# The low parts of 22 weight units move from VectorE to GpSimd, and the final norm's chunks are put between them

## The chip, the cores and the metric

One core of one Trainium2 chip runs the whole program. The metric is the device time in microseconds (us). The engines are named as in the profile: PE is TensorE (PEld its weight loads), DVE VectorE, ACT ScalarE, POOL GpSimd, SP SyncE.

## The reference

Two blocks of two layers each, float32, model width 1024, 256 tokens. The first block has feed-forward layers and two mixers, and ends with a final norm. The second puts 16 meta tokens ahead (272 rows) and runs `hybrid_layer` twice; the change lies here:

```python
def hybrid_layer(x, ...):
    h = rms_norm_2(x, norm_g)
    z = h @ w_in
    aq, ak, av, ag, mq, mk, mv, mi, mf, mo, mgate = jnp.split(z, split_points(), axis=-1)
    ...
    ya = sliding_window_sink_attention(q, k, v, sink) * jax.nn.silu(ag)
    ...
    hm = mlstm_chunkwise(mq, mk, mv, log_i, log_f)
    ym = rms_norm_2(hm, out_norm_g) * jax.nn.sigmoid(mo) * jax.nn.silu(mgate)
    y = jnp.concatenate([ya, ym], axis=-1) @ w_out
    return x + y
```

The attention has 16 heads of 64, the mLSTM 4 heads (q and k of 128, v of 256).

## The kernel before

Every weight matrix is cut into units of 512 rows by 256 columns (128 partitions x 4 x 256 in SBUF); there are 456. A unit U passes through four engines: SP loads it into `raw[U % 4]`; ACT copies it, rounded, into the high part `w_hi` (L1124, semaphore `hi_made`); DVE subtracts the two and leaves the low part `w_lo` (L1862, `split_w`, semaphore `lo_made`); PE multiplies hi by the activations' high and low parts and lo by the high part (L690). In the second block the high and low parts have five slots, of which one lies in `y_both`, so that a group named `y_both<-raw` is the same work as `w_lo<-raw`. The slot of `raw` is loaded again once the low part is made.

Units 320 to 371 and 388 to 439 are the streams of the two hybrid layers: 52 units each, numbered u = 0 to 51 below, in the order kv, mif, aq, mqk, mv, mo, ag, mg. Behind each come 16 units of the projection (u = 52 and on). All engines walk through the same list; in step u, ACT and DVE make the parts of unit u + 4 (`split_ahead`, `units_ahead`). A table `VISITS` says which pieces of attention and mLSTM each step does beside its unit: attention in u = 18 to 34 (`att`), the four mLSTM heads in u = 34 to 51 (`ml`, stages 0 to 3 of head k in steps 34, 36, 37, 39 plus 4k).

One mLSTM head is a loop over the engines. Its lines, as the prediction names them: ACT takes squares of PE's sums (L1558, L1560), PE sums those (L1056), DVE adds (L2446), ACT takes a root (L1578, with a table load at L1156 before it), DVE inverts (L2458) and scales (L2469), DVE makes the next head's matrix (L2420, L2432, L2434) for PE (L1047). The gates of mo, ag and mg run in between on the same engines: DVE scales a tile from PSUM (L1899), multiplies (L2451, L2481, then L2489 or L2494), ACT rounds the result into `y_both` (L1594), DVE makes its low part (L2504). DVE and ACT run everything in the written order.

GpSimd in these steps scales attention rows (L1808, L1810) and, behind all visits of layer 0, multiplies the eight chunks of `h` for the final norm (L1838, L1839, chained by `link`); DVE waits for them (`h_final`) only in the projection.

Of the kernel before, what the change touches and what calls it, by code (L numbers as in the profile page):

```python
# [192 lines left out]
    return U - RING - 1  # L193


def units_ahead(U):

    u = U - FIRST_STREAM
    if u < CATCH_UP:
        return (U + LEAD,)  # L200
    return (U + LEAD, U + LEAD + 1) if u == CATCH_UP else (U + LEAD + 1,)
# [51 lines left out]
def build_stack(nc: bass.Bass, consts, x, ffn1_norm, ffn1_w_in, ffn1_w_out, mix_norm, ffn2_norm, ffn2_w_in, ffn2_w_out,  # L253
# [12 lines left out]
    with ExitStack() as ctx:  # L266
# [3 lines left out]
        def sem(name):  # L270
            return ctx.enter_context(nc.semaphore(name))
# [37 lines left out]

        ident, tri = cst("ident"), cst("tri")  # L310

        def hi_part(U):
            s = parts_slot(U)
            return parts_5[0] if s == RING else w_hi[:, s]

        def lo_part(U):
            s = parts_slot(U)
            return parts_5[1] if s == RING else w_lo[:, s]
# [82 lines left out]
        w_loaded = [sem(f"w_loaded{i}") for i in range(RING)]  # L401
        hi_made = sem("hi_made")
        lo_made = sem("lo_made")
        unit_done = sem("unit_done")
        first_done = sem("first_done")
        tile_read = sem("tile_read")
# [104 lines left out]
        def _(sp):  # L511
# [23 lines left out]
            def load(U, src, wait):  # L535

                n = UNITS[U][3]
                if wait is not None:
                    sp.wait_ge(lo_made, wait)
                sp.dma_start(raw[:, U % RING, 0:n, :], src).then_inc(w_loaded[U % RING], 16)  # L540

# [17 lines left out]
            def straight(name, first=0):  # L559
                ub, pb, npairs = PHASES[name]  # L560
                for p in range(first, npairs):
                    for U in units_before(name, p):
                        src, l, k0, n, c0 = UNITS[U]
                        a = dram[src][l]
                        if name == "out01":

                            for dst, s_ in small[2 * (U - ub):2 * (U - ub) + 2]:
                                sp.dma_start(dst, s_).then_inc(sg_loaded, 16)
                        if name.startswith("mif"):

                            sp.wait_ge(lo_made, U - RING + 1)
                            for g in range(2):
                                sp.dma_start(raw[:, U % RING, 0:n, 32 * g:32 * g + 4],
                                             a[k0 * P:(k0 + n) * P, c0 + 4 * g:c0 + 4 * g + 4].rearrange(
                                                 "(k p) n -> p k n", p=P)).then_inc(w_loaded[U % RING], 16)
                            continue
                        load(U, a[k0 * P:(k0 + n) * P, c0:c0 + CU].rearrange("(k p) n -> p k n", p=P),
                             U - RING + 1 if U >= RING else None)
# [56 lines left out]
        def _(pe):  # L635
# [12 lines left out]
            def unit(U, k0, n, pair, npair_off, xs, N, first, last, ready, off, tiles=2, wide_x=False,  # L648
                     mid=None, both=False):


                pe.wait_ge(lo_made, U + 1 + off)
                hi_w, lo_w = hi_part(U), lo_part(U)
                accs = [bank[tile_bank(2 * pair + m, off)] for m in range(tiles)]

                def bank_free(m):

                    T = 2 * pair + m
                    if T in BANK_OF:
                        pe.wait_ge(gates_sig, 2 * NC8)  # L660
                        if T >= 2 * PHASES["sg_out"][1]:
                            pe.wait_ge(sg_read, NC8)
                        if BANK_OF[T] < 4:
                            pe.wait_ge(tile_read, T - 7)
                    elif T in FIRST_BANK and isinstance(off, int) and off == 0:
                        pe.wait_ge(tile_read, T - 7)
                    elif not isinstance(off, int):
                        pe.wait_ge(halves_added, TURNED[T] - 3 + tile_off(off))
                    elif not (T - 3 + off // 2 <= 0):
                        pe.wait_ge(tile_read, T - 3 + tile_off(off))  # L670

                for j in range(n):
                    k = k0 + j
                    if ready is not None:
                        pe.wait_ge(act_ready, ready + k + 1)
                    a, b = (k * L + META, (k + 1) * L) if N == SEQ and wide_x else (k * N, (k + 1) * N)
                    begin, end = first and j == 0, last and j == n - 1
                    residual = 2 * pair in T_OUT
                    if both:
                        kinds = ((hi_w, xs[:, :, a:b], slice(0, 2 * N)), (lo_w, xs[:, 0, a:b], slice(N, 2 * N)))  # L680
                    else:
                        kinds = tuple((w, xs[:, i, a:b], slice(0, N)) for w, i in ((hi_w, 0), (hi_w, 1), (lo_w, 0)))
                    for g, (w, moving, cols) in enumerate(kinds):
                        final = end and g == len(kinds) - 1
                        for m in range(tiles):
                            if begin and g == 0:
                                bank_free(m)
                                if residual and BANK_OF[2 * pair + m] < 4:
                                    add_residual(2 * pair + m)
                            i_ = mm(accs[m][:, cols], w[:, j, m * P:(m + 1) * P], moving,  # L690
                                    start=begin and g == 0 and not residual, stop=final)
                            if final and m == 0 and tiles == 2:
                                i_.then_inc(first_done, 1)
                    if j == n // 2 - 1 and mid is not None:
                        mid()
                i_.then_inc(unit_done, 1)
# [984 lines left out]
        def _(pool):  # L1681
# [113 lines left out]
            for l in range(DEPTH):  # L1795
# [16 lines left out]
                def turn(c):  # L1812
# [13 lines left out]
                    if c == NC8:  # L1826
                        pool.wait_ge(qc_new, n + 1)
                        pool.wait_ge(rs_new, l + 1)
                        nc.gpsimd.memset(k_up[:, :, :], 0.0).then_inc(padded, 1)

                for u in range(STREAM_UNITS):
                    for kind, n in VISITS[u]:
                        if kind in ("att", "turn"):
                            dict(att=att, turn=turn)[kind](n)
                if l == 0:
                    pool.wait_ge(final_r, 1)
                    for c in range(NC8):
                        link(nc.gpsimd.tensor_scalar(h[:, c, META:L], h[:, c, META:L], pcol("final_norm", c), None, MUL))  # L1838
                        TT(h[:, c, META:L], h[:, c, META:L], sq[:, META:L], MUL).then_inc(h_final, 1)  # L1839
                    pool.wait_ge(h_final, NC8)  # L1840
                    h_squares(7, "proj0", 0)

# [2 lines left out]
        def _(dve):  # L1845
# [10 lines left out]
            def split_w(U, off=0):  # L1856

                if U >= NU:
                    return
                n, s = UNITS[U][3], U % RING  # L1860
                dve.wait_ge(hi_made, U + 1 + off)
# [795 lines left out]
```

## Time and profile before

| | |
|---|---|
| median of 3 runs | 1449.24 us (1448.88 to 1450.42) |
| the profiled execution's own time | 1448.88 us |
| its span in the profile | 1447.1 us |
| PE busy | 1432.7 us, 99% of the span |
| DVE busy | 1092.7 us, 76% |
| ACT busy | 853.7 us, 59% |
| POOL busy | 273.1 us, 19% |

The span is 1.8 us shorter than the execution's own time. A busy share is an average over stages. In the timeline an instruction that waits for access to its operands is still shown as running, so its duration against that of its like tells of such a wait.

### The profile page before, as it was taken

What the parts mean: (1) busy time and instruction counts of PE and PEld (TensorE: products, weight loads), DVE (VectorE), ACT (ScalarE), POOL (GpSimd) and SP (SyncE); (2) the same over time, 40 slices, a digit from 0 to 9 for tenths busy, and PEclk for the clock granted to TensorE, in tenths of its full rate; (3) what the DMA queues carried; (4) which work ended last, traced back from release to release, by engine and by line L of the source; (5) the groups of instructions that cost most, each with busy time, mean ns of one, the idle gap of its engine ahead of it and who ended that gap; (6) DMA issues with size and microseconds to landing.
All of it is one profiled execution on the core that took longest, in us unless ns stands there. A gap on an engine that the chain in (4) does not pass through costs nothing.

```text
span 1447.1 us, 27343 instructions
## 1 busy us (share of the span) xinstructions
PE 1432.7 (99%) x9657; PEld 1321.4 (91%) x9657; DVE 1092.7 (76%) x2021; ACT 853.7 (59%) x1559; POOL 273.1 (19%) x329
## 2 busy tenths in 40 slices
PE   8999999999999999999999999999999999999998
PEld 7888899988888888889988888999999999999998
DVE  6777679877756777667787766898778779976883
ACT  6665458766544666446566554656757555576762
POOL 1111113121102111014031113332250035121000
PEclk9999999999999999999999999999999999999999
DMA  6667754556565656565456565554345555434533
GB/s 211 196 196 211 233 180 131 186 179 202 183 188 182 191 187 198 186 195 164 159 171 201 181 188 175 164 145 124 88 127 142 164 153 155 134 94 124 147 118 117
DMA packets 247875, 241.25 MB, mean 167 GB/s; under 512 B 15456, under 2 KB 246736, under 8 KB 247784
## 3 DMA queue, kind: packets, MB, share of 16 engines
q1 hardware_dynamic: 244888, 236.73, 53.8%
q10 hardware_dynamic: 2896, 3.30, 0.8%
q8 instruction: 58, 0.95, 0.3%
q14 instruction: 33, 0.27, 0.1%
HBM read 238.92 MB, written 1.07 MB: 166 GB/s over the span
## 4 chain that ended last, share of the span: by engine, by line
PE 87%; DVE 7%; ACT 3%; issue 2%; DMA 1%; ACTq 0%; SPq 0%; DVEq 0%
PE bank L690 78%; DVE w_lo L1862 2%; DVE work L2458 1%; PE bank L989 1%; ACT w_hi L1124 1%; PE bank L1007 1%; PE bank L972 1%; PE bank L918 1%; DMA raw<-in_w_out_dram 1%; PE bank L928 1%; DVE work L1899 1%; DVE work L2481 1%; DMA raw<-in_ffn_w_in_dram 1%; PE bank L988 1%; ACT L1156 0%
## 5 line engine op out<-in xcount | busy, mean ns | idle before, releaser
L690 PE MATMUL bank<-x_both,w_hi 128*128 128x512 f32 (+2 forms) x3216 | 748.1, 336 | 0.6 <-DVE h L1962 0.5
L1862 DVE TENSOR_TENSOR w_lo<-raw,w_hi 128x1024 fp32r<-128x1024 f32 (+1 forms) x429 | 519.4, 1234 | 203.3 <-ACT w_hi L1124 202.2
L1124 ACT CAST w_hi<-raw 128x1024 fp32r<-128x1024 f32 (+1 forms) x429 | 429.3, 1028 | 125.4 <-PE bank L690 108.3
L690 PEld LDWEIGHTS bank<-x_both,w_hi 128*128 128x128 f32 x3216 | 468.0, 189 | 3.5 <-DVE w_lo L1862 1.1
L690 PEld LDWEIGHTS bank<-x_both,w_lo 128*128 128x128 f32 x2312 | 406.1, 189 | 62.7
L690 PE MATMUL bank<-x_both,w_lo 128*128 128x256 f32 (+1 forms) x2312 | 462.4, 281 | 0.0
L690 PE MATMUL bank<-y_both,w_hi 128*128 128x512 f32 (+2 forms) x1376 | 331.5, 342 | 1.8 <-DVE w_lo L1862 1.1
L690 PEld LDWEIGHTS bank<-y_both,w_lo 128*128 128x128 f32 x1040 | 184.3, 188 | 31.3
L690 PE MATMUL bank<-y_both,w_lo 128*128 128x256 f32 (+1 forms) x1040 | 206.1, 280 | 0.0
L690 PEld LDWEIGHTS bank<-y_both,w_hi 128*128 128x128 f32 x1376 | 200.3, 189 | 2.8 <-DVE w_lo L1862 1.8
L1749 POOL TENSOR_TENSOR work<-work,rstd 128x256 f32<-128x256 f32 x88 | 67.0, 783 | 412.7 <-ACT work L1193 412.7
L1175 ACT COPY pre<-bank 128x256 f32<-128x256 f32 x176 | 56.7, 374 | 67.1 <-PE bank L690 66.8
L1205 ACT CAST y_both<-work 128x256 f32 (+1 forms) x88 | 32.7, 406 | 59.7 <-DVE work L1930 59.5
L690 PE MATMUL bank<-x_both,y_both 128*128 128x272 f32 (+1 forms) x504 | 67.6, 290 | 0.0
L1193 ACT ACTIVATE work<-work 128x256 f32<-128x256 f32 x88 | 33.2, 418 | 53.4 <-DVE work L1919 53.4
L1135 ACT ACTIVATE x_both<-h,par 128x256 fp32r<-128x256 f32 (+1 forms) x56 | 28.2, 513 | 61.2 <-DVE h L1975 52.9
L690 PEld LDWEIGHTS bank<-x_both,y_both 128*128 128x128 f32 x504 | 63.6, 188 | 0.6
L1810 POOL TENSOR_SCALAR work<-work 128x256 f32<-128x256 f32 x32 | 36.4, 1137 | 99.2 <-DVE work L2381 99.2
L1714 POOL TENSOR_TENSOR sq<-h 128x256 f32<-128x256 f32 (+1 forms) x34 | 21.4, 631 | 163.2 <-DVE h L1975 162.9
L1879 DVE SCALAR_TENSOR_TENSOR x_both<-h,par,x_both 128x256 fp32r<-128x256 f32 (+1 forms) x56 | 29.1, 528 | 24.8 <-ACT x_both L1135 24.6
L1937 DVE TENSOR_TENSOR y_both<-work,y_both 128x256 f32 (+1 forms) x88 | 33.6, 423 | 15.3 <-ACT y_both L1205 14.7
L1899 DVE TENSOR_TENSOR work<-bank,rstd 128x256 f32<-128x256 f32 (+1 forms) x98 | 37.5, 422 | 6.8 <-PE bank L690 6.5
(312 smaller groups left out, 1397.9 us busy)
## 6 DMA issues: line engine op xcount, KB each, us to landing
raw<-in_ffn_w_in_dram SPq DMA_DIRECT2D x176, 512.0 KB, 3.8
raw<-in_w_in_dram SPq DMA_DIRECT2D x100, 512.0 KB, 3.7
raw<-in_ffn_w_out_dram SPq DMA_DIRECT2D x64, 512.0 KB, 4.6
raw<-in_w_out_dram SPq DMA_DIRECT2D x32, 512.0 KB, 4.0
raw<-in_ffn_w_out_dram SPq DMA_DIRECT2D x32, 384.0 KB, 3.4
raw<-in_rec_w_in_dram SPq DMA_DIRECT2D x16, 512.0 KB, 4.4
raw<-in_sg_w_in_dram SPq DMA_DIRECT2D x16, 512.0 KB, 4.1
raw<-in_rec_w_out_dram SPq DMA_DIRECT2D x8, 512.0 KB, 3.5
```

The costliest lines, as they stand in the source:

```text
L690: i_ = mm(accs[m][:, cols], w[:, j, m * P:(m + 1) * P], moving, start=begin and g == 0 and not residual, stop=final)
L1124: nc.scalar.copy(hi_part(U)[:, 0:n, :], raw[:, s, 0:n, :]).then_inc(hi_made, 1)
L1135: i_ = activation(xview(dst, k, N), src, ACT.Copy, scale=scale)
L1175: nc.scalar.copy(ffn_b[:, m, :], bank[b][:, SEQ:2 * SEQ]).then_inc(low_copied, 1)
L1193: activation(ffn_s[:, m, :], ffn_t[:, m, :], ACT.Silu).then_inc(silu_done, 1)
L1205: nc.scalar.copy(dst, ffn_h[:, m, :]).then_inc(act_hi, 1)
L1749: TT(ffn_r[:, m, :], ffn_s[:, m, :], rstd[:, META:L], MUL).then_inc(gate_scaled, 1)
L1810: TS(pr[:, P:AW], pr[:, P:AW], rec[:, 1:2], None, MUL).then_inc(s_prob, 1)
L1862: TT(lo_part(U)[:, 0:n, :], raw[:, s, 0:n, :], hi_part(U)[:, 0:n, :].bitcast(fp32), SUB).then_inc(lo_made, 1)
L1879: i_ = STT(out=xview(dst_lo, k, N), in0=src, scalar=scale, in1=hi, op0=MUL, op1=SUB)
L1899: TT(dst, tile(pr, m, N), rstd[:, T0:L], MUL).then_inc(tile_read, 1)
L1937: TT(lo, ffn_h[:, m, :], hi.bitcast(fp32), SUB).then_inc(act_ready, 1)
```

## The change

Eleven units of each stream (u = 23, 26, 29, ... 53, the last of them in the projection) get their low part from GpSimd. DVE skips them. GpSimd makes each in the step four before (19, 22, ... 49), after that step's attention work, and counts them on a semaphore of its own, `lo_by_pool`; PE and SP wait on that one for these units and on `lo_made` for the rest. The eight chunks of the final norm, which stood behind the last visit of layer 0, now stand one in each of the steps 36 to 43, behind the step's low part.

```diff
+POOL_UNITS = [FIRST_STREAM + l * (STREAM_UNITS + 16) + u for l in range(DEPTH) for u in range(23, 54, 3)]
+
+def parts_made(U):
+
+    made = sum(V < U for V in POOL_UNITS)
+    return (1, made + 1) if U in POOL_UNITS else (0, U + 1 - made)
...
+        def wait_parts(engine, U):
+            by_pool, count = parts_made(U)
+            engine.wait_ge(lo_by_pool if by_pool else lo_made, count)
...
@@ block.sync, load @@
-                if wait is not None:
+                if wait is not None and isinstance(wait, int):
+                    wait_parts(sp, wait - 1)
+                elif wait is not None:
                     sp.wait_ge(lo_made, wait)
...
@@ block.tensor, unit @@
-                pe.wait_ge(lo_made, U + 1 + off)
+                if isinstance(off, int):
+                    wait_parts(pe, U + off)
+                else:
+                    pe.wait_ge(lo_made, U + 1 + off)
...
@@ block.gpsimd @@
+                def low_part(U):
+
+                    if U in POOL_UNITS:
+                        pool.wait_ge(hi_made, U + 1)
+                        TT(lo_part(U), raw[:, U % RING], hi_part(U).bitcast(fp32), SUB).then_inc(lo_by_pool, 1)
+
                 for u in range(STREAM_UNITS):
                     for kind, n in VISITS[u]:
                         if kind in ("att", "turn"):
                             dict(att=att, turn=turn)[kind](n)
-                if l == 0:
-                    pool.wait_ge(final_r, 1)
-                    for c in range(NC8):
+                    low_part(FIRST_STREAM + l * (STREAM_UNITS + 16) + u + LEAD + 1)
+                    if l == 0 and 36 <= u < 36 + NC8:
+                        c = u - 36
+                        if c == 0:
+                            pool.wait_ge(final_r, 1)
                         link(nc.gpsimd.tensor_scalar(h[:, c, META:L], h[:, c, META:L], pcol("final_norm", c), None, MUL))
                         TT(h[:, c, META:L], h[:, c, META:L], sq[:, META:L], MUL).then_inc(h_final, 1)
+                if l == 0:
                     pool.wait_ge(h_final, NC8)
                     h_squares(7, "proj0", 0)
...
@@ block.vector, split_w @@
                 if U >= NU:
                     return
+                if U in POOL_UNITS:
+                    return
```

In the changed file the lines stand further down: GpSimd's L1838 and L1839 are L1865 and L1866 there, the new low part is L1854, DVE's L1862 is L1892 and its lines behind that are 30 higher.

GpSimd's queue in layer 0, from the end of its attention work into the mLSTM steps, before:

```order
L1810 TENSOR_SCALAR work<-work 128x256 [waits s_rec] x8
L1838 TENSOR_SCALAR h<-h,par 128x256 [waits final_r]
L1839 TENSOR_TENSOR h<-h,sq 128x256 [waits pool_ch]
L1838 TENSOR_SCALAR h<-h,par 128x256
L1839 TENSOR_TENSOR h<-h,sq 128x256 [waits pool_ch]
```

and of the change, from the low part of u = 38 on:

```order
L1854 TENSOR_TENSOR w_lo<-raw,w_hi 128x1024 [waits hi_made]
L1865 TENSOR_SCALAR h<-h,par 128x256 [waits final_r]
L1866 TENSOR_TENSOR h<-h,sq 128x256 [waits pool_ch]
L1854 TENSOR_TENSOR w_lo<-raw,w_hi 128x1024 [waits hi_made]
L1865 TENSOR_SCALAR h<-h,par 128x256
L1866 TENSOR_TENSOR h<-h,sq 128x256 [waits pool_ch]
L1865 TENSOR_SCALAR h<-h,par 128x256
L1866 TENSOR_TENSOR h<-h,sq 128x256 [waits pool_ch]
L1865 TENSOR_SCALAR h<-h,par 128x256
L1866 TENSOR_TENSOR h<-h,sq 128x256 [waits pool_ch]
L1854 TENSOR_TENSOR y_both<-raw,y_both 128x1024 [waits hi_made]
L1865 TENSOR_SCALAR h<-h,par 128x256
```

Chunk 0 now stands behind the low part of u = 38, chunks 1 to 3 behind that of u = 41, chunks 4 to 6 behind that of u = 44 and chunk 7 behind that of u = 47.

DVE's queue in layer 1 around step 40, before, from the tiles of step 39 to the low part of u = 45:

```order
L1899 TENSOR_TENSOR work<-bank,rstd 128x256 [waits unit_done]
L2451 SCALAR_TENSOR_TENSOR work<-work 128x256 [waits gate_act] x2
L2481 SCALAR_TENSOR_TENSOR work<-work 128x256 [waits gate_act] x2
L2489 SCALAR_TENSOR_TENSOR work<-work 128x256 [waits s_out,dch]
L2489 SCALAR_TENSOR_TENSOR work<-work 128x256
L1862 TENSOR_TENSOR w_lo<-raw,w_hi 128x1024 [waits hi_made]
L2504 TENSOR_TENSOR y_both<-work,y_both 128x256 [waits act_hi] x2
L2441 TENSOR_TENSOR work<-work 128x272 [waits floor_loaded,m_dsq,m_num]
L1862 TENSOR_TENSOR w_lo<-raw,w_hi 128x1024 [waits hi_made]
```

and of the change:

```order
L1929 TENSOR_TENSOR work<-bank,rstd 128x256 [waits unit_done]
L2481 SCALAR_TENSOR_TENSOR work<-work 128x256 [waits gate_act] x2
L2511 SCALAR_TENSOR_TENSOR work<-work 128x256 [waits gate_act] x2
L2519 SCALAR_TENSOR_TENSOR work<-work 128x256 [waits s_out,dch]
L2519 SCALAR_TENSOR_TENSOR work<-work 128x256
L2534 TENSOR_TENSOR y_both<-work,y_both 128x256 [waits act_hi] x2
L2471 TENSOR_TENSOR work<-work 128x272 [waits floor_loaded,m_dsq,m_num]
L1892 TENSOR_TENSOR w_lo<-raw,w_hi 128x1024 [waits hi_made]
```

The low part of u = 44 is gone from behind the gate's products; that of u = 45 stays.

## Rows read from the trace of the kernel before

**Rows 1.** The page: busy time of each engine, and the chain by engine

```profile
PE 1432.7 (99%) x9657; PEld 1321.4 (91%) x9657; DVE 1092.7 (76%) x2021; ACT 853.7 (59%) x1559; POOL 273.1 (19%) x329
...
PE 87%; DVE 7%; ACT 3%; issue 2%; DMA 1%; ACTq 0%; SPq 0%; DVEq 0%
```

**Rows 2.** Windows of 10 us: PE, PEld, DVE, ACT, POOL busy, granted clock, DMA

```profile
1360.00:1370.00 10.00, 9.28 (x70) 8.68 (x69) 9.84 (x22) 6.70 (x15) 0.00 (x0) 1.00 0.43 119
1380.00:1390.00 10.00, 9.09 (x70) 8.57 (x69) 9.84 (x22) 5.43 (x13) 0.00 (x0) 1.00 0.53 162
1400.00:1410.00 10.00, 8.94 (x76) 8.73 (x75) 7.88 (x14) 6.23 (x9) 0.00 (x0) 1.00 0.29 80
...
1120.00:1130.00 10.00, 9.61 (x74) 9.24 (x73) 7.39 (x16) 7.78 (x15) 0.00 (x0) 1.00 0.50 157
1150.00:1160.00 10.00, 9.50 (x76) 9.29 (x75) 6.40 (x11) 4.39 (x7) 4.16 (x6) 1.00 0.75 248
```

**Rows 3.** The chain that ended last, layer 0 and layer 1: start, us, what

```profile
1093.00 1.86 DVE work L2458
...
1357.05 1.86 DVE work L2458
...
1366.99 0.44 DVE work L2489
1367.45 0.67 ACT y_both L1594 x2
...
1374.32 1.86 DVE work L2458
```

**Rows 4.** Timeline of POOL: start, us, engine, line, operation

```profile
1057.48 0.92 POOL L1838 TENSOR_SCALAR h<-h,par 128x256 f32<-128x256 f32 x1
1058.49 0.73 POOL L1839 TENSOR_TENSOR h<-h,sq 128x256 f32<-128x256 f32 x1
...
1191.44 0.78 POOL L1825 TENSOR_TENSOR work<-work 128x272 f32<-128x272 f32 x1
```

**Rows 5.** Timeline of DVE and of POOL, layer 1, query turns beside low parts

```profile
1201.23 1.22 DVE L1862 TENSOR_TENSOR w_lo<-raw,w_hi 128x1024 fp32r<-128x1024 f32 x1
1202.37 1.69 DVE L1862 TENSOR_TENSOR y_both<-raw,y_both 128x1024 fp32r<-128x1024 f32 x1
...
1201.46 1.51 POOL L1824 TENSOR_TENSOR work<-work,con 128x272 f32<-128x272 f32 x1 [3.11 <-DVE work L2312]
1202.93 1.76 POOL L1825 TENSOR_TENSOR work<-work 128x272 f32<-128x272 f32 x1
```

**Rows 6.** Timeline of ACT and of DVE, layer 1, step 40

```profile
1348.71 1.03 ACT L1124 CAST w_hi<-raw 128x1024 fp32r<-128x1024 f32 x1
...
1349.73 0.76 DVE L2489 SCALAR_TENSOR_TENSOR work<-work 128x256 f32<-128x256 f32 x2
1350.40 1.22 DVE L1862 TENSOR_TENSOR w_lo<-raw,w_hi 128x1024 fp32r<-128x1024 f32 x1
```

**Rows 7.** Timeline of ACT and of DVE, layer 1, step 43

```profile
1361.79 1.04 ACT L1124 CAST w_hi<-raw 128x1024 fp32r<-128x1024 f32 x1
...
1363.08 0.74 DVE L2504 TENSOR_TENSOR y_both<-work,y_both 128x256 fp32r<-128x256 f32 x2
```

**Rows 8.** Timeline of ACT and of DVE, layer 1, step 46

```profile
1375.71 1.04 ACT L1124 CAST w_hi<-raw 128x1024 fp32r<-128x1024 f32 x1
...
1377.15 0.76 DVE L2481 SCALAR_TENSOR_TENSOR work<-work 128x256 f32<-128x256 f32 x2
```

**Rows 9.** Timeline of DVE, layer 1, step 49

```profile
1387.30 1.23 DVE L1862 TENSOR_TENSOR w_lo<-raw,w_hi 128x1024 fp32r<-128x1024 f32 x1
1388.44 0.75 DVE L1899 TENSOR_TENSOR work<-bank,rstd 128x256 f32<-128x256 f32 x2
```

**Rows 10.** Timeline of POOL and of DVE, attention of layer 0

```profile
1004.78 1.02 POOL L1810 TENSOR_SCALAR work<-work 128x256 f32<-128x256 f32 x1 [2.83 <-DVE work L2381]
...
1009.18 0.16 DVE L2380 TENSOR_TENSOR work<-work 128x2 f32<-128x2 f32 x1
```

More of the change, by code:

```diff
@@ L403, in build_stack @@
         lo_made = sem("lo_made")
+        lo_by_pool = sem("lo_by_pool")
         unit_done = sem("unit_done")
@@ L569, in straight @@
                         if name.startswith("mif"):
-                            sp.wait_ge(lo_made, U - RING + 1)
+                            wait_parts(sp, U - RING)
                             for g in range(2):
```

## The prediction

> **What bounds the kernel now.** I read the page first: PE is busy 99% of the span, and 87% of the chain that ended last is PE [rows 1]. So the most that any change off PE can give is what PE waits. The windows say where that is: five stretches of 10 us, all at the end of a stream, in which PE is busy 9.28, 9.09, 8.94, 9.61 and 9.50 of 10 [rows 2]; the missing parts sum to 0.72 + 0.91 + 1.06 + 0.39 + 0.50 = 3.6 us. In two of them DVE is busy 9.84 of 10. Then the chain: in both layers it leaves PE in the mLSTM steps and goes round DVE and ACT, once per head. DVE inverts at 1357.05 and again at 1374.32, a loop of 17.27 us, and within it goes straight from DVE's gate product (L2489) to ACT's rounding (L1594) [rows 3]. ACT takes its squares behind that, and PE's L1056 waits for them. So there are two regimes. In attention and in the projections' bulk PE is the bound and DVE has room. In steps 38 to 52 of each stream the bound is the DVE and ACT loop: a microsecond more or less on DVE between two inversions is a microsecond of the end, once PE's small cover is used up, and at both layers' ends it is, since PE waits there.
>
> **What the change removes.** 22 low parts leave DVE. The next instruction starts 1.14 us behind such a one [rows 5], so DVE sheds 25 us of work. Which of them are on the loop decides. Six of eleven per layer (u = 23 to 38) are made in steps 19 to 34, attention. There DVE waits for ACT's exponentials anyway: worth nothing. The other five are made in steps 37, 40, 43, 46 and 49, in the loop.
>
> **What it adds.** First the operation's own time. GpSimd takes 0.73 us for a product of 256 columns and 0.78 for 272 [rows 4]; it never did 1024 columns or this rounded output. If 0.16 us of it is fixed, as DVE shows for two columns [rows 10], the rest grows fourfold: 0.16 + 4 x 0.57 = 2.4 us. Bounds: nothing fixed, 4 x 0.73 = 2.9; half fixed, 0.37 + 4 x 0.37 = 1.8. I take 2.4. GpSimd has room: its work share is 19% [rows 1], and PE needs each part four steps later, over 10 us.
>
> The Trainium skill (GPSIMD Engine Reference, section 3.1) gives 4497 ns for a float32 tensor_tensor of 2048 columns; half of it, an estimate from that page, is 2.25 us. By it the sum below would be 0.9 us lower.
>
> Second, the lock. GpSimd's L1824 starts at 1201.46 while DVE's low part runs, and takes 1.51 us, where its like take under 0.8; it ends at 1202.97. DVE's next low part starts at 1202.37 and takes 1.69 instead of 1.22: the other's rest was 0.60, it lost 0.47, so a blocked instruction loses the rest less 0.13. GpSimd's next one (1202.93) again takes 1.76 [rows 5]. So they exclude each other for whole instructions, and take turns: GpSimd, waiting first, went ahead of the DVE instruction queued behind. DVE instructions with one operand in PSUM do not seem to take part. The price is then not the 1.1 us that DVE sheds but what stands behind the 2.4 us that GpSimd holds.
>
> The Trainium skill (SBUF — State Buffer, section SBUF: two separate sides) says that a DVE instruction with two SBUF inputs and a GpSimd instruction that reads SBUF share an exclusive lock, and that the later one fully blocks. By that rule the sum is the one below; without a lock it would be the first rival. The trace agrees with its 1.69 us for 1.22.
>
> **Where each low part lands**, from layer 1 (layer 0 has the same order):
> - Attention: GpSimd is free at 1005.80 and would run to 1008.2; DVE's next instruction with two SBUF operands is at 1009.18 [rows 10]. Cost 0. After the double step 22 it falls on later ones, but with PE's slack of some microseconds there.
> - Step 37: DVE's tile scaling (PSUM, not blocked) may start earlier, but PE's tile is only just done: -0.3, bounds 0 and -1.1.
> - Step 40: ACT ends the high part of u = 44 at 1349.74. DVE starts the first of two gate products at 1349.73 and the second right behind [rows 6]. GpSimd waits for the first, then goes ahead of the second: +2.25 (2.4 less 0.13). The low part shed here (1350.40) stood behind L1594's release and off the loop: nothing comes back. L1594, the squares, the next high part and PE's L1056 are late by all of it.
> - Step 43: the high part is ready at 1362.83, while DVE makes the low part of u = 46. GpSimd goes next and holds up L2504, due at 1363.08 [rows 7]: +2.25, less the 1.13 of the low part shed before the tiles: +1.1.
> - Step 46: ready at 1376.75, GpSimd runs to 1379.25. L2481 was due at 1377.15 [rows 8]: +1.95. Less 1.13 is +0.8; ACT's next high part is late by the full 1.95 and then sets DVE's low part of u = 51: +1.0.
> - Step 49: DVE's low part (1387.30) stood between the loop and the tiles at 1388.44 [rows 9]; the tiles read PSUM: -1.15.
>
> Sum per layer -0.3 + 2.25 + 1.1 + 1.0 - 1.15 = +2.9; both layers +5.8.
>
> **The final norm's chunks** (layer 0 alone) ran in steps 36 to 39, beside DVE work that PE covered. Each is 0.92 + 0.73 us of GpSimd [rows 4]. Chunks 1 to 3 now run behind the low part of u = 41, beside L2420 and L2481: +0.3. Chunks 4 to 6 follow that of u = 44, where DVE has L2504 twice and L2441: turns of 0.92, 0.73 and 0.92 less 0.13 each are 2.2, the fourth turn ahead of the low part of u = 45 adds 0.6, and 1.3 is idle time in which DVE waited for that unit's high part: +1.5. Chunk 7 takes one turn: +0.8. Together +2.6, bounds 0 and 4.0. The final norm itself is due only in the projection, and is early enough.
>
> SP's loads wait for parts that are ready up to 3 us later, with more than 5 us to spare before ACT needs them: 0. PE and SP get no more instructions.
>
> Total +8.4. Against the profiled execution's own 1448.88 (span 1447.1) that is 1457.3; the median stood 0.36 above it, and I forecast 1457.4.
>
> **Bounds.** The operation's time enters six blocks (steps 40, 43, 46 twice): 6 x -0.6 = -3.6 and 6 x +0.5 = +3.0. Chunks: -2.6 to +1.4. Low end 1457.3 - 6.2 = 1451.1, high end 1461.7.
>
> **Rivals.**
> - No lock between these two forms, or so short that it doesn't matter (for it: most of the low parts beside GpSimd's work show small differences; against: [rows 5]). Then steps 37, 43, 46 and 49 shed 3.7 us per layer from the loop, and PE stops waiting: at most the 3.6 us of [rows 2], 1445.3. It decides if a low part on DVE beside GpSimd's stays at 1.22. Chance 0.10.
> - The lock is real but the blocks miss the loop. The point is step 40: if GpSimd starts 0.75 us later than I think, both gate products have passed, and 2.25 per layer go away: +3.9 in all; if the chunks find DVE waiting too, +1.3, which is 1450.2. Against it: [rows 6], start and end within 0.01 us, and either order ends at the same time. Chance 0.14.
> - The main case, DVE blocked on its loop: 0.76, of which some 0.04 lies above the range through effects in attention (a GpSimd row scaling late by a low part, and PE's transposes with it).
>
> This kernel's runs tell a change from none at about 0.2%, 2.9 us. The main case is slower, the second rival within, the first faster. The range must leave out the first rival and a little at the top: 1450.5 to 1462.5.
>
> **What would show it.** In the profile after: GpSimd's low parts at 2.4 us when alone. DVE's busy time down by less than 25 us, since blocked instructions count as running. The second L2519 of step 40 (L2489 before) at about 2.7 us instead of 0.43, L2534 in step 43 and L2511 in step 46 likewise. PE's waits before its squares' sum (L1056 before) up from under 1 us to 1 to 4 us in the last three heads of both layers, the loop of 17.27 us at 19 or more for heads 1 to 2 and 18.4 for the next, and the attention steps unchanged. I am wrong if these blocks are short, if DVE goes ahead of a waiting GpSimd, or if GpSimd's operation takes much less or more than 1.8 to 2.9 us.

## The result, and the profile after

The changed kernel takes 1455.13 us (median of 6 runs, 1453.82 to 1455.98), the kernel before 1449.21 us in the same series (6 runs, 1448.56 to 1450.42). The ratio is 1.004, with a 95% interval of 1.003 to 1.005: slower by 5.9 us. The profiled execution took 1454.83 us, its span is 1453.0 us. Forecast were 1457.4 us and "slower"; the time lies in the range.

The page of the changed kernel first, its line of busy times and the group of GpSimd's low parts:

```profile
PE 1432.9 (99%) x9657; PEld 1321.0 (91%) x9657; DVE 1084.8 (75%) x1999; ACT 853.8 (59%) x1559; POOL 326.0 (22%) x351
...
L1854 POOL TENSOR_TENSOR w_lo<-raw,w_hi 128x1024 fp32r<-128x1024 f32 x18 | 44.8, 2487 | 88.1 <-ACT w_hi L1143 88.1
```

DVE lost 22 instructions that take 1.14 us each from start to start, 25 us, but its busy time fell by only 7.9 us against [rows 1]: the rest is DVE standing in front of a lock, which counts as running. Then the waits of PE (line, for whom, us in total, times, longest), after:

```profile
PE bank L1075 <- ACT work L1577: 5.5, 4, 1.7
PE bank L1066 <- DVE work L2464: 3.3, 2, 1.9
```

In the kernel before, the first of these was

```profile
PE bank L1056 <- ACT work L1558: 2.0, 3, 0.9
```

and the second was not there. Both lie in the mLSTM steps at the ends of the two streams.

The loop of the heads shows where. DVE's inversion (L2458 before, L2488 after) stands once in each head. The timeline of DVE, the kernel before, layer 0 and layer 1 (the inversions of [rows 3] not repeated), and one row of attention in layer 1 for the offset:

```profile
1075.46 1.85 DVE L2458 RECIPROCAL work<-work 128x272 f32<-128x272 f32 x1 [1.26 <-ACT work L1578]
1110.54 1.85 DVE L2458 RECIPROCAL work<-work 128x272 f32<-128x272 f32 x1 [1.51 <-ACT work L1578]
1133.46 1.84 DVE L2458 RECIPROCAL work<-work 128x272 f32<-128x272 f32 x1
...
1248.13 0.17 DVE L2381 RECIPROCAL work<-work 128x2 f32<-128x2 f32 x1
1339.79 1.85 DVE L2458 RECIPROCAL work<-work 128x272 f32<-128x272 f32 x1 [1.42 <-ACT work L1578]
...
1396.91 1.84 DVE L2458 RECIPROCAL work<-work 128x272 f32<-128x272 f32 x1
```

and the same of the changed kernel:

```profile
1075.18 1.85 DVE L2488 RECIPROCAL work<-work 128x272 f32<-128x272 f32 x1 [0.96 <-ACT work L1597]
1095.49 1.85 DVE L2488 RECIPROCAL work<-work 128x272 f32<-128x272 f32 x1 [1.50 <-ACT work L1597]
1114.04 1.85 DVE L2488 RECIPROCAL work<-work 128x272 f32<-128x272 f32 x1 [1.51 <-ACT work L1597]
1136.67 1.84 DVE L2488 RECIPROCAL work<-work 128x272 f32<-128x272 f32 x1
...
1251.68 0.17 DVE L2411 RECIPROCAL work<-work 128x2 f32<-128x2 f32 x1
...
1343.06 1.85 DVE L2488 RECIPROCAL work<-work 128x272 f32<-128x272 f32 x1 [1.06 <-ACT work L1597]
1362.52 1.85 DVE L2488 RECIPROCAL work<-work 128x272 f32<-128x272 f32 x1 [1.04 <-ACT work L1597]
1380.19 1.85 DVE L2488 RECIPROCAL work<-work 128x272 f32<-128x272 f32 x1 [1.50 <-ACT work L1597]
...
1402.51 1.84 DVE L2488 RECIPROCAL work<-work 128x272 f32<-128x272 f32 x1
```

The reader takes the distance between two inversions in each list and subtracts. Through attention the two executions keep one distance: the changed one is 0.17 us early in layer 0 and 3.55 late in layer 1 (1251.68 less 1248.13), so its layer 0 had cost 3.7 by then. The one exception seen is two rows of layer 0 (L2411 at 1001.03 and 1004.88), 0.36 us late behind a low part of GpSimd; at the next row, 1009.22, the distance is back. From there:

| | predicted | layer 0 | layer 1 |
|---|---|---|---|
| up to the first inversion (step 37) | -0.3 | -0.11 | -0.28 |
| first to second (step 40) | +2.25 | +2.77 | +2.20 |
| second to third (step 43) | +1.1 | +1.01 | +0.40 |
| third to fourth (steps 46, 49) | +1.0 - 1.15 | -0.29 | -0.27 |
| behind the fourth, to the end | 0 | +0.34 | +0.30 |
| sum | +2.9, and +2.6 for chunks in layer 0 | +3.7 | +2.35 |

Layer 0 has the chunks in it. Now the blocks, as the text calls the time that an instruction stands in front of the lock. The timelines of POOL and of DVE in step 40 of layer 1, changed kernel:

```profile
1353.08 2.60 POOL L1854 TENSOR_TENSOR w_lo<-raw,w_hi 128x1024 fp32r<-128x1024 f32 x1 [11.52 <-ACT w_hi L1143]
...
1352.99 2.97 DVE L2519 SCALAR_TENSOR_TENSOR work<-work 128x256 f32<-128x256 f32 x2
...
1357.44 0.44 DVE L2471 TENSOR_TENSOR work<-work 128x272 f32<-128x272 f32 x1 [0.58 <-ACT work L1579]
1358.31 1.22 DVE L1892 TENSOR_TENSOR w_lo<-raw,w_hi 128x1024 fp32r<-128x1024 f32 x1 [0.43 <-ACT w_hi L1143]
```

Beside [rows 6]: the pair L2519 took 0.76 us and now takes 2.97. The second of the pair began 0.34 in, so it took 2.63 where it takes 0.42. Step 43 of layer 1 went otherwise:

```profile
1368.38 3.17 POOL L1854 TENSOR_TENSOR w_lo<-raw,w_hi 128x1024 fp32r<-128x1024 f32 x1 [12.70 <-ACT w_hi L1143]
...
1367.41 1.20 DVE L1892 TENSOR_TENSOR y_both<-raw,y_both 128x1024 fp32r<-128x1024 f32 x1
1368.54 0.74 DVE L2534 TENSOR_TENSOR y_both<-work,y_both 128x256 fp32r<-128x256 f32 x2
1369.21 0.74 DVE L1929 TENSOR_TENSOR work<-bank,rstd 128x256 f32<-128x256 f32 x2
1369.88 2.28 DVE L2481 SCALAR_TENSOR_TENSOR work<-work 128x256 f32<-128x256 f32 x2
```

GpSimd was shown as running from 1368.38, but both L2534 (0.74 us, as always) passed it. Its 3.17 us are 0.8 of waiting and 2.4 of work, and of this only what outlasted the tiles from PSUM fell on DVE: L2481 (L2451 before) took 2.28 instead of 0.74, 1.54 us. Less the 1.14 of the low part shed that is +0.40. In layer 0 the same block is followed by chunk 7:

```profile
1102.98 2.27 DVE L2481 SCALAR_TENSOR_TENSOR work<-work 128x272 f32<-128x272 f32 x2
1105.17 0.98 DVE L2511 SCALAR_TENSOR_TENSOR work<-work 128x272 f32<-128x272 f32 x2
1106.18 1.24 DVE L2519 SCALAR_TENSOR_TENSOR work<-work 128x272 f32<-128x272 f32 x2
...
1078.01 1.36 DVE L2511 SCALAR_TENSOR_TENSOR work<-work 128x272 f32<-128x272 f32 x2
...
1077.98 0.74 POOL L1866 TENSOR_TENSOR h<-h,sq 128x256 f32<-128x256 f32 x1
1088.54 1.39 POOL L1865 TENSOR_SCALAR h<-h,par 128x256 f32<-128x256 f32 x1
...
1091.92 1.14 POOL L1866 TENSOR_TENSOR h<-h,sq 128x256 f32<-128x256 f32 x1
```

L2511 and L2519 lost 0.2 and 0.45 us there, 0.65 for chunk 7. The L2511 of 1.36 us is that of step 38, beside the second half of chunk 3: it takes 0.79 alone, so chunk 3 cost 0.57, which is all by which layer 0's +2.77 exceeds layer 1's +2.20. The last two POOL rows are of chunks 4 and 5: with these it was mostly GpSimd that waited (0.92 and 0.73 us alone).

### The profile page after: what moved, and what is told of

The parts are those of the page before. It is cut to its first block, busy times and chain, and to the rows that moved or that the text cites. A ratio compares the mean times of both kernels' runs of the same rounds, so it can differ in the third digit from the quotient of the medians.

```text
span 1453.0 us, 27343 instructions
## 1 busy us (share of the span) xinstructions
PE 1432.9 (99%) x9657; PEld 1321.0 (91%) x9657; DVE 1084.8 (75%) x1999; ACT 853.8 (59%) x1559; POOL 326.0 (22%) x351
## 4 chain that ended last, share of the span: by engine, by line
PE 90%; DVE 5%; ACT 2%; issue 2%; DMA 1%; ACTq 0%; SPq 0%; DVEq 0%
PE bank L709 81%; DVE w_lo L1892 1%; PE bank L1008 1%; PE bank L1026 1%; DVE work L2488 1%; PE bank L991 1%; PE bank L937 1%; PE bank L947 1%; DVE work L2519 1%; DMA raw<-in_ffn_w_in_dram 1%; ACT w_hi L1143 1%; PE bank L1007 1%; PE bank L1066 1%; DVE work L1929 0%; PE bank L1027 0%
## 5 line engine op out<-in xcount | busy, mean ns | idle before, releaser
L1892 DVE TENSOR_TENSOR w_lo<-raw,w_hi 128x1024 fp32r<-128x1024 f32 (+1 forms) x411 | 497.5, 1235 | 202.4 <-ACT w_hi L1143 201.7
L1854 POOL TENSOR_TENSOR w_lo<-raw,w_hi 128x1024 fp32r<-128x1024 f32 x18 | 44.8, 2487 | 88.1 <-ACT w_hi L1143 88.1
```

Source lines behind the costliest of these rows:

```text
L1854: TT(lo_part(U), raw[:, U % RING], hi_part(U).bitcast(fp32), SUB).then_inc(lo_by_pool, 1)
L1892: TT(lo_part(U)[:, 0:n, :], raw[:, s, 0:n, :], hi_part(U)[:, 0:n, :].bitcast(fp32), SUB).then_inc(lo_made, 1)
```

## The experiments

All twelve are built on the changed kernel and timed against the kernel before on the same chip; "against before" is the difference to its median in that series (1448.6 to 1450.0 us). The changed kernel's own is +5.9. Between two series the differences to before are compared, not the bare medians. Where a run's file has one to three lines more, its line numbers are that much higher (L2521 in experiment 6 is L2519).

**1. Only attention's low parts** (the list `range(23, 54, 3)` of units cut):

```diff
-POOL_UNITS = [... for u in range(23, 54, 3)]
+POOL_UNITS = [... for u in range(23, 39, 3)]
```

> The changed kernel with only the six low parts per layer that are made in attention (u = 23 to 38, steps 19 to 34) on GpSimd; the five in the mLSTM steps go back to DVE. My theory: attention costs nothing, so the time is that of the kernel before, 1449.2 us, within 1. In the changed kernel the high parts stood 0.17 us early all through layer 0's attention and a constant 3.55 late all through layer 1's, which is what the theory rests on. Rival: part of the 5.9 us is made in attention, by GpSimd scaling rows later: 1451 to 1453.

Measured: 1448.66 us, ratio 0.9999 (0.9990 to 1.0008). Attention costs nothing and gives nothing, though DVE sheds 12 low parts there. The chunks keep their new places in this run, and with no low part ahead of them they cost nothing either.

**2. The same places, one input.** The low parts of these 22 units are left out (they are zero).

```diff
-TT(lo_part(U), raw[:, U % RING], hi_part(U).bitcast(fp32), SUB).then_inc(lo_by_pool, 1)
+nc.gpsimd.tensor_scalar(lo_part(U), raw[:, U % RING], 0.0, None, MUL).then_inc(lo_by_pool, 1)
```

> The changed kernel with the same 22 instructions on GpSimd at the same places and waits, but each reads one tensor (a TENSOR_SCALAR of raw times 0) instead of two: the low parts of these units are left out of the products (they are zero). Theory of the lock between instructions with two operands in SBUF: in the changed kernel L1865, a TENSOR_SCALAR, ran beside DVE's low part (1091.22, 1.24 us) and beside L2450 without holding either up, so here the blocks of L2519, L2511 and L2481 go away, at whatever length the GpSimd instruction has, and DVE is rid of 22 low parts: 1445.3 to 1447 us. Rival: any long GpSimd instruction on SBUF keeps DVE out, or the loss comes from the order of waits and not from a lock: 1454 or more.

Measured: 1446.54 us, ratio 0.9984 (0.9975 to 0.9993). Queue, waits and places are those of the changed kernel, and GpSimd's instruction is even longer (2.77 us alone), yet the loss is gone and turns into a gain of 2.4 us. So the loss hangs on what GpSimd's instruction is, not on the waits or the order. The run changes its operation together with the number of its inputs; which of the two decides is not separated here. Step 40 of layer 1, DVE and POOL:

```profile
1349.14 1.60 DVE L2519 SCALAR_TENSOR_TENSOR work<-work 128x256 f32<-128x256 f32 x2
...
1349.24 2.96 POOL L1854 TENSOR_SCALAR w_lo<-raw 128x1024 fp32r<-128x1024 f32 x1 [11.12 <-ACT w_hi L1143]
```

L2519 loses 0.84 us, not 2.2: this instruction keeps DVE out for a part of its time only, and its last 1.5 us run beside DVE's next ones. It is not free, though: L2511 in step 46 took 1.32 us for 0.75, and L2481 in step 43 0.92 for 0.74. That the blocks would go away at any length, as I expected, did not hold.

**3. Step 40 alone undone**, and **4. the same with the chunks back in step 36.**

```diff
-... for u in range(23, 54, 3)]
+... for u in range(23, 54, 3) if u != 44]
```

> The changed kernel with one unit per layer (u = 44, made in step 40) back on DVE, so 20 low parts on GpSimd instead of 22. My theory: the block of the second L2519 (2.63 us instead of 0.42) is the whole price of step 40, 2.2 us per layer, and the later steps stay as they are: 1455.1 - 4.4 = 1450.7 us, within 1. Rival: the loop is bound elsewhere too (ACT's table loads, PE's sums), so that a block taken away shows only in part, or the next block grows by as much: 1453 to 1455.

Measured: 1452.23 us, ratio 1.0023 (1.0014 to 1.0033), 3.3 against before. That is 2.6 less than the changed kernel (2.9 by the bare medians), not 4.4. In the trace layer 1 gave 1.9 back and layer 0 only 1.15; from first to second inversion it was the full 2.2 in layer 1. The timelines of layer 0 there show the chunks, which used to run in the shadow of the low part's block, now taking turns with DVE on the loop:

```profile
1081.90 2.17 POOL L1865 TENSOR_SCALAR h<-h,par 128x256 f32<-128x256 f32 x1
...
1082.94 0.98 DVE L2534 TENSOR_TENSOR y_both<-work,y_both 128x272 fp32r<-128x272 f32 x2
...
1086.58 1.35 DVE L2511 SCALAR_TENSOR_TENSOR work<-work 128x272 f32<-128x272 f32 x2
```

> The changed kernel with u = 44 back on DVE and, as well, the chunks all in step 36. Taking away u = 44 alone gave 2.9 us where 4.4 were expected: in layer 1 1.9 of the 2.2, in layer 0 only 1.15. In that run's trace GpSimd's chunks, which had run while the low part's block kept DVE waiting, now took turns with DVE's own instructions from step 38 on (L2534 0.63 for 0.43, L2511 1.00 for 0.43). Theory: without them layer 0 gains what layer 1 does: 1454.2 (chunks alone back) less 2 x 1.9 = 1450.4, 1449.6 to 1451.2. Rival: in layer 0 the block of step 40 was partly covered by PE's slack whatever the chunks do: 1451.5 to 1452.5.

Measured: 1449.46 us, ratio 1.0001 (0.9993 to 1.0010). That is just below my range of 1449.6 to 1451.2. Against the run that has only the chunks back (experiment 5) it is 5.3 less (4.7 by the bare medians). From first to second inversion the step itself gives 2.2 us in either layer when the chunks are out of the way. With step 40 and the chunks' spread undone, nothing of the slowdown is left that can be measured.

**5. The chunks alone back in step 36.**

```diff
-if l == 0 and 36 <= u < 36 + NC8:
-    c = u - 36
-    if c == 0:
-        pool.wait_ge(final_r, 1)
-    link(...); TT(...)
+if l == 0 and u == 36:
+    pool.wait_ge(final_r, 1)
+    for c in range(NC8):
+        link(...); TT(...)
```

> The changed kernel with the eight chunks of the final norm all in step 36, ahead of the low part of u = 41, where they ran in the kernel before. By the recorded prediction their spreading costs 2.6 us: 1452.5. By the trace of the changed kernel layer 0 cost 3.7 and layer 1, which has no chunks, 2.4: 1.3 at most for the chunks, of it 0.65 at chunk 7 (L2511 0.63 for 0.43 and L2519 0.89 for 0.43 us); chunks 4 to 6 ran while GpSimd, not DVE, waited. So 1453.9, 1453.3 to 1454.6. In the trace the shift against the kernel before should grow equally in both layers.

Measured: 1454.18 us, ratio 1.0036 (1.0022 to 1.0050). That is 5.6 against before, 0.3 under the changed kernel's, with intervals that overlap, so the times alone show no gain; the trace is finer: layer 0 cost 2.5 us in place of 3.7. So by the traces the spread costs 1.2 us, not 2.6. Layer 1 ended 0.7 later than in the changed kernel, all of it behind its last head, which I can't explain.

**6. GpSimd waits for both products in step 40.**

```diff
 pool.wait_ge(hi_made, U + 1)
+if (U - FIRST_STREAM) % (STREAM_UNITS + 16) == 44:
+    pool.wait_ge(act_new, 16 + 16 * l + 4)
```

> The changed kernel, in which GpSimd's low part of u = 44 (step 40) waits until DVE has made the gate's second product, so that this product is never held up. The prediction's second rival took it that 2.25 us per layer would then go away: 1455.1 - 4.4 = 1450.7. My theory now is that DVE runs in order and every one of its instructions with two SBUF operands ahead of the tiles is on the loop: L2534 is held up in place of L2519, and only the idle time behind it is saved (0.58 us ahead of L2471 and 0.43 ahead of the next low part, since ACT's rounding comes earlier), about 1.0 per layer: 1453.1, from 1452.3 to 1454.

Measured: 1453.15 us, ratio 1.0029 (1.0019 to 1.0040), 4.6 against before. The timeline of DVE, step 40 of layer 1:

```profile
1352.14 0.76 DVE L2521 SCALAR_TENSOR_TENSOR work<-work 128x256 f32<-128x256 f32 x2
1353.04 2.95 DVE L2536 TENSOR_TENSOR y_both<-work,y_both 128x256 fp32r<-128x256 f32 x2
```

The products are free (0.76 us) and L2536, the later L2534, takes the block. What is won is the idle time ahead of L2471 and of the low part in the changed kernel's rows above, 1.0 us per layer by those rows (1.0 and 1.2 from first to second inversion). The recorded second rival, which let the 2.25 us vanish once the products had passed, had that wrong: everything that DVE does ahead of the tiles is on the loop.

**7. Each low part in two halves of 512 columns.**

```diff
-TT(lo_part(U), raw[:, U % RING], hi_part(U).bitcast(fp32), SUB).then_inc(lo_by_pool, 1)
+TT(lo_part(U)[:, 0:2, :], raw[:, U % RING, 0:2, :], hi_part(U)[:, 0:2, :].bitcast(fp32), SUB)
+TT(lo_part(U)[:, 2:4, :], raw[:, U % RING, 2:4, :], hi_part(U)[:, 2:4, :].bitcast(fp32), SUB).then_inc(lo_by_pool, 1)
```

> The changed kernel with every low part of GpSimd made by two instructions of 512 columns each, so that the lock is given up in the middle. If the two engines take turns for whole instructions, the second L2519 of step 40 waits for one half (about 1.2 us) and L2534 behind it for the other, the sum stays 2.2 us, and the time 1455, within 1. Rival: DVE, which has its next instruction ready, goes on with several before GpSimd's second half gets in, and that half falls on DVE's tiles from PSUM, which it doesn't hold up: 1.1 us less in each of steps 40 and 46, 1451 to 1452.5.

Measured: 1453.77 us, ratio 1.0033 (1.0021 to 1.0046), 5.2 against before, between what the theory and its rival said. Step 40 of layer 1:

```profile
1351.91 1.86 DVE L2520 SCALAR_TENSOR_TENSOR work<-work 128x256 f32<-128x256 f32 x2
1353.70 1.84 DVE L2535 TENSOR_TENSOR y_both<-work,y_both 128x256 fp32r<-128x256 f32 x2
...
1352.00 1.49 POOL L1854 TENSOR_TENSOR w_lo<-raw,w_hi 128x512 fp32r<-128x512 f32 x1 [11.37 <-ACT w_hi L1143]
1353.45 1.47 POOL L1855 TENSOR_TENSOR w_lo<-raw,w_hi 128x512 fp32r<-128x512 f32 x1
```

Here they alternate strictly, one half and one DVE instruction. The two blocks sum to the one of before (1.1 + 1.1), but the second product comes 1.1 us earlier, and with it ACT's rounding, which takes away idle time as in experiment 6.

**8. GpSimd asks 0.2 us later in step 43.**

```diff
 pool.wait_ge(hi_made, U + 1)
+if (U - FIRST_STREAM) % (STREAM_UNITS + 16) == 47:
+    nc.gpsimd.memset(pause[:, :], 0.0)
```

> The changed kernel, in which GpSimd clears 48 columns of a tile of its own (0.14 us for such a MEMSET in the changed kernel's trace) between its wait and the low part of u = 47 (step 43), so that it asks about 0.2 us later. In the changed kernel it started there 0.17 us ahead of DVE's L2534 (1368.376 against 1368.543) and both L2534 went first; in step 40, where it started 0.25 us ahead of DVE's next (1353.081 against 1353.333), it went first itself. Theory: the one that has asked by the time that the lock comes free gets it, and GpSimd needs about 0.2 us from its start in the trace to ask. Then it now stands 0.3 us ahead of the second L2534, goes before it, and that one takes about 2.6 us; the block then costs 2.2 less 1.1 (as recorded) instead of the 0.4 of layer 1: 0.7 us per layer more, 1456.5, from 1455.8 to 1457.2. Rival: a pair of DVE instructions that stand ready is not broken into here; GpSimd starts behind the pair again, the block of L2481 grows by nothing, and the time stays 1455.1, or falls on L2481 0.1 later.

Measured: 1455.30 us, 5.3 against before (ratio 1.0034, 1.0022 to 1.0046). My theory fell:

```profile
1368.43 0.14 POOL L1856 MEMSET pause<- 128x48 f32 x1 [12.68 <-ACT w_hi L1144]
1368.53 3.08 POOL L1857 TENSOR_TENSOR w_lo<-raw,w_hi 128x1024 fp32r<-128x1024 f32 x1
...
1368.61 0.74 DVE L2537 TENSOR_TENSOR y_both<-work,y_both 128x256 fp32r<-128x256 f32 x2
...
1369.95 2.27 DVE L2484 SCALAR_TENSOR_TENSOR work<-work 128x256 f32<-128x256 f32 x2
```

GpSimd shows as running 0.42 us ahead of the second L2537 (the pair's second began at 1368.95) and still stands behind it. The changed kernel's own rows spoke against the theory already: GpSimd started there 0.5 us ahead of the second L2534 (1368.38 against 1368.88). The rival, that a pair that stands ready is not broken into, fits step 43 but not step 40, where the second L2519 waits for no semaphore and GpSimd went before it. In experiment 6 GpSimd (start 1353.04) went between the two L2536 (0.43 and 2.61 us), but there the second was not ready: ACT's rounding for it ended at 1353.34.

**9. The bad place, three times a layer** (in the mLSTM steps u = 44, 48 and 52 only), and **10. the good place** (u = 41, 45, 49 and 53 only).

```diff
-... for u in range(23, 54, 3)]
+... for u in (*range(23, 39, 3), 44, 48, 52)]
```

> The counterpart of the run with u = 41, 45, 49 and 53: here GpSimd makes, beside the six of attention, u = 44, 48 and 52 (steps 40, 44 and 48). All three stand where step 40 does in a head's loop: in the kernel before, ACT ended the high part of u = 48 at 1367.01 beside L2489 at 1366.99, and that of u = 52 at 1384.29 beside L2494 at 1384.26. Theory that the place decides: each costs 2.2 us as step 40 did, 6.6 per layer, 13.2 in both, less about 1 for the cover PE still has at the first: 1461.5 us, 1459.5 to 1463. Rival: what counts is how many are moved (6 here in the loops against 10 in the changed kernel, which cost 5.9): 1452 to 1454.

Measured: 1461.90 us, ratio 1.0091 (1.0077 to 1.0105), 13.3 against before. By the distances of the inversions and ACT's high parts each of the six cost 2.15 to 2.22 us, 13.1 together. The last, step 48 of layer 1:

```profile
1394.79 2.96 DVE L2524 TENSOR_TENSOR work<-work 128x256 f32<-128x256 f32 x2
```

```diff
-... for u in range(23, 54, 3)]
+... for u in (*range(23, 39, 3), 41, 45, 49, 53)]
```

> The changed kernel with other units on GpSimd in the mLSTM steps: u = 41, 45, 49 and 53, made in steps 37, 41, 45 and 49, in place of 41, 44, 47, 50 and 53. All of them stand at the same place of a head's loop, where DVE goes from its low part to the tiles from PSUM. My theory: it is the place in the loop that decides, not the work moved. Step 49 gave 1.3 us and step 37 gave 0.3 in the changed kernel; steps 41 and 45 should give 1.1 to 1.3 each as step 49 does. That is 2.7 to 3.2 per layer, but no more than PE waits there (3.6 us in both layers together): 1446 us, from 1445.3 to 1447.5. Rival: the gain of step 49 is special to the last head, behind which no next matrix is made; in steps 41 and 45 GpSimd holds up L2450, the three additions for the next head (two operands in SBUF), by up to 1.2 us each and nothing is won: 1449 to 1451.

Measured: 1442.53 us, ratio 0.9959 (0.9946 to 0.9973), 6.4 faster than before, and better than I held possible. DVE and POOL in step 41 of layer 1 and behind:

```profile
1351.70 1.74 DVE L2450 TENSOR_TENSOR work<-work,con 128x128 f32<-128x128 f32 x3
1353.36 1.85 DVE L2488 RECIPROCAL work<-work 128x272 f32<-128x272 f32 x1
...
1369.21 1.84 DVE L2488 RECIPROCAL work<-work 128x272 f32<-128x272 f32 x1
...
1350.61 2.39 POOL L1854 TENSOR_TENSOR w_lo<-raw,w_hi 128x1024 fp32r<-128x1024 f32 x1 [14.58 <-ACT w_hi L1143]
```

The loop is 15.85 us instead of 17.27. L2450 is held up (1.74 us for 0.56), as the rival said, but before, DVE sat idle at that point for ACT's root (1.51 us ahead of the inversion at 1110.54, and as much in layer 1), and the inversion now follows with no idle time. The windows of PE, before and in this run (the first number behind the window is its length, then PE's busy time and its instructions):

```profile
1370.00:1390.00 20.00, 19.09 (x150) 18.29 (x149) 18.13 (x38) 13.37 (x29) 0.00 (x0) 1.00 0.48 143
```

```profile
1370.00:1390.00 20.00, 20.00 (x162) 19.57 (x161) 18.11 (x36) 15.40 (x31) 2.39 (x1) 1.00 0.42 135
```

PE's missing 0.91 us are gone, but 12 instructions more stand in the window, 8%. It isn't the same piece of the program to the instruction, so I take the totals: over the whole span, with 9657 instructions in both, PE's idle time fell from 14.4 to 10.3 us and its busy time from 1432.7 to 1430.4. The idle time alone fell by 4.1 us, so the 3.6 us of [rows 2] that I took for the most that PE could win were too few. The other 2.3 us suggest that the busy time of before had waiting in it: with the same instructions it is 1436.0 us in experiment 9, where the loops are longest. It isn't proven by the pair alone, since experiment 1, as fast as before, has 1431.5.

**11. The good place alone**, without attention's units and with the chunks in step 36, 8 units in all.

```diff
-... for u in range(23, 54, 3)]
+... for u in (41, 45, 49, 53)]
```

> Only the low parts of u = 41, 45, 49 and 53 on GpSimd (8 in both layers, none in attention), and the chunks of the final norm all in step 36 as before. If attention's moves and the spreading of the chunks give nothing, this is as fast as the run that had the same four and six more in attention (1442.5): 1442.5 us, 1441.8 to 1443.3. Rival: the attention's low parts do help PE somewhere once it is the bound: 1443.5 to 1445.

Measured: 1443.19 us, ratio 0.9955 (0.9942 to 0.9968), 6.0 faster than before. Attention and the spread add nothing that can be measured.

**12. Step 49 alone**, with the chunks in step 36 as in experiments 4, 5 and 11. The expectation says that they stand in their new places; the run's edit puts them back.

```diff
-... for u in range(23, 54, 3)]
+... for u in (53,)]
```

> Only the low part of u = 53 (step 49) on GpSimd, in both layers; the chunks in their new places, which with nothing before them on GpSimd are as early as before. The recorded prediction's term is -1.15 per layer, the changed kernel's trace -1.3. Without the other four the loop is less late, so PE's cover counts for more; before, PE missed 0.39 + 0.50 us in the windows at layer 0's end and 1.06 us in the one at layer 1's: 1.2 to 2.4 us of gain in all, 1447.2, from 1446.5 to 1448.

Measured: 1446.93 us, ratio 0.9982 (0.9974 to 0.9991), 2.3 faster than before: 1.1 per layer, the recorded term. Only the times of this run are used.

## Why the prediction was right, by its own steps

**The bound, and attention: right.** The loop of DVE and ACT at the streams' ends took all of the loss, attention none (experiment 1). In layer 1 the loops took 19.46 and 17.67 us, forecast were 19 or more and 18.4.

**The operation's time: right.** Predicted 2.4 us (1.8 to 2.9), measured 2.36 to 2.41 where GpSimd was alone. The halves took 1.27 to 1.30 each, so some 0.18 us are fixed (2 x 1.28 less 2.38), where I had assumed 0.16. The Trainium skill (GPSIMD Engine Reference, section 3.1) led to 2.25 by halving its figure; the trace is 0.1 above that.

**The lock: right, and shown.** Beside the 2.4 us instruction DVE's second L2519 took 2.63 us for 0.42, and with the same queue and one input less the loss turned into a gain (experiment 2). A blocked instruction lost the rest less 0.14 (L2519 ended 0.28 behind GpSimd, and takes 0.42). The Trainium skill (SBUF — State Buffer, section SBUF: two separate sides) holds the pair locked against two-input DVE work for the whole of any GpSimd instruction that reads SBUF. The blocks of L2519, L2511 and L2481 agree with it for GpSimd's instruction with two inputs; its TENSOR_SCALAR does not agree, it cost L2519 0.84 us of its 2.96.

**Step 37: right.** -0.3 predicted, -0.28 in layer 1 and -0.11 in layer 0.

**Step 40: right.** +2.25 predicted, +2.20 in layer 1 by the loop and in layer 0 without chunk 3, and 2.2 per layer when it is undone (experiment 4). The six blocks of experiment 9 are the same.

**Step 43: the lock right, the order wrong, and with it the size.** The step read "GpSimd goes next and holds up L2504 ...: +2.25, less the 1.13 ...: +1.1". GpSimd did not go next; DVE's pair went first and the block shrank to what was left behind the tiles, 1.54 - 1.14 = +0.40. The +1.01 of layer 0 holds 0.6 for chunk 7 (+0.35 in experiment 5, without it). I had taken the turn order for a rule from two rows [rows 5], and "if DVE goes ahead of a waiting GpSimd" was one of the recorded signs of being wrong: for this step it came true.

**Steps 46 and 49: right.** Together -0.15 predicted, -0.29 and -0.27 measured. The pair L2511 took 2.69 us in step 46 (0.75 before, +1.94; predicted +1.95). In step 49 I had overlooked a block:

```profile
1383.03 2.69 DVE L2511 SCALAR_TENSOR_TENSOR work<-work 128x256 f32<-128x256 f32 x2
...
1395.04 2.26 DVE L2511 SCALAR_TENSOR_TENSOR work<-work 128x256 f32<-128x256 f32 x2
```

The second row is step 49, 1.5 us of block behind the tiles, but there DVE has 1.46 us of idle time ahead of its next low part, and the gain stayed.

**The final norm's chunks: the mis-sized term.** Predicted +2.6 (+0.3 for chunks 1 to 3, +1.5 for 4 to 6, +0.8 for 7). Measured 1.2 by the trace of experiment 5: by the loop's rows 0.57 up to the second inversion and 0.6 for chunk 7. The 0.57 are chunk 3's, ahead of step 40; chunks 4 to 6 cost the loop nothing. Of the recorded working, "turns of 0.92, 0.73 and 0.92" is what failed for chunks 4 to 6: half of a chunk is a TENSOR_SCALAR, which here hardly kept DVE out (1.24 us for the low part beside it, 1.23 before), for most of the time GpSimd did the waiting, and the idle time that the low part's block had just made on DVE took in the rest (0.17 us ahead of its next low part in layer 0, 0.43 in layer 1). Experiments 3 and 4 show the other side: without that block the chunks cost about 1 us more.

**The sum.** 8.4 predicted. Less 1.4 for the chunks, 0.7 for step 43 in each layer, 0.25 for steps 46 and 49, 0.05 for step 40 in each layer, and 0.17 by which the execution was early at the start of layer 0; plus 0.64 behind the last heads and 0.2 at step 37. That makes 5.9, and the spans differ by 5.9. That the forecast came this near is in part luck: the 0.64, for which it had no term, made up for some of the 2.8 us by which the chunks and step 43 were too high. The 0.64 stay open: between kernels what is lost or won behind the last head ran from -0.6 to +1.2 us, and no run was aimed at it. In layer 0 it isn't noise: it was +0.30 to +0.35 in all eight traces with step 49's low part on GpSimd beside the others of the changed kernel, +1.2 in experiments 10 and 11, and +0.04 and -0.14 in experiments 1 and 9, which leave step 49 to DVE. It looks as if part of what is won ahead of the fourth inversion is not kept there.

**The rivals.** No lock: excluded by the blocks and by experiment 2, though its price was about right (1446.5 for 1445.3). Blocks that miss the loop: the point named, GpSimd 0.75 us later in step 40, was tried in experiment 6, and gives 1.0 per layer, not 2.25.

## What to carry to other kernels

Before work is moved to GpSimd, look at what DVE does in the microseconds behind the start: with two SBUF inputs on both sides DVE stops for the whole instruction, and whether that costs is decided by the place in the loop. The same instruction cost 2.2 us a piece beside the gate's products and won 0.9 in layer 0 and 1.4 in layer 1 (experiment 11, steps 41, 45 and 49, from one inversion to the next) where DVE was about to read PSUM and then to wait for ACT. A period (every third unit) that doesn't match the loop's (four steps) hits each place in turn, and the sum hides both. PE's idle time was no bound for the gain here: count its instructions in the window too.

## What the runs showed that I had not expected

- Who goes first at the lock is no plain alternation. In step 40 GpSimd, shown as running 0.25 us ahead of DVE's next instruction, went before it; in step 43 both instructions of a pair passed it, though it was shown 0.17 us ahead of the first and 0.5 ahead of the second (0.08 and 0.42 in experiment 8); in experiment 6 it went between the two of such a pair, the second of which was not ready yet; in halves the two alternated strictly. What decides is open.
- GpSimd's TENSOR_SCALAR of 1024 columns takes longer than its TENSOR_TENSOR (2.77 against 2.36 us) and yet holds DVE up less: 0.84, 0.18 and 0.57 us in steps 40, 43 and 46 of layer 1.
- With the same 9657 instructions PE's busy time went from 1430.4 us (experiment 10, short loops) over 1432.7 (before) to 1436.0 (experiment 9, long loops), so part of a wait seems to be booked as PE's work. Experiment 1 with 1431.5 shows a spread of about 1 us without any change of the loop.
